# Gate projections moved into the latent attention, their logits carried through DRAM, and inverse roots spread by transposes

## The reference, cut to what matters

```python
fq, fk, fv, f_logit, c_q, c_kv, k_rope, gate_logit = split(u @ w_in)
o_fox = attention(fq, fk, fv, ...) @ w_branch_fox
q = rms_norm(heads(rms_norm(c_q) @ w_uq));  k, v = heads(rms_norm(c_kv) @ w_ukv)  # k normed with k_rope
o_mla = attention(rope(q), rope(k), v) @ w_branch_mla
g_fox, g_mla = split(sigmoid(gate_logit + b_gate))            # 1024 + 1024 columns
h = h + (g_fox * o_fox + g_mla * o_mla) @ w_out
```

## Time and profile before

| | us |
|---|---|
| median of 3 runs | 2599.38 (2598.16 to 2601.02) |
| the profiled execution | 2598.46 |
| its span, first to last instruction | 2596.3 |
| PE busy | 2433.0 (94%) |
| DVE, ACT, POOL busy | 1418.0, 948.2, 557.8 |
| mean granted TensorE clock | 0.958 of 2.4 GHz |

### The profile page before, as it was taken

The page is one execution under the profiler, slowest core; times in us unless marked ns, Lnnn a source line. Parts: engine busy times, 40 slices in busy tenths (PEclk is TensorE's granted clock), DMA queues, the critical chain, the costliest instruction groups (busy, mean ns, idle before and its releaser), DMA issues. The chain is left out here.

```text
span 2596.3 us, 37171 instructions
## 1 busy us (share of the span) xinstructions
PE 2433.0 (94%) x14204; PEld 2152.8 (83%) x14204; DVE 1418.0 (55%) x2006; ACT 948.2 (37%) x1578; POOL 557.8 (21%) x655
## 2 busy tenths in 40 slices
PE   6999999999959999978999998999998999999999
PEld 6899999999958888976777777888876888887887
DVE  7665655565456567544666662111466666655553
ACT  5333333333344445432444443111334333334332
POOL 0023300000023344231444444222310333000000
PEclk8999999999979999987998998999999999999999
DMA  4365632565230000010000002111433566326653
GB/s 183 121 209 196 209 114 95 214 227 188 101 130 1 26 26 0 1 33 7 7 7 4 3 1 81 48 49 41 163 113 104 180 221 232 133 87 255 211 197 111
DMA packets 125908, 281.13 MB, mean 108 GB/s; under 512 B 9456, under 2 KB 56432, under 8 KB 122432
## 3 DMA queue, kind: packets, MB, share of 16 engines
q1 hardware_dynamic: 125760, 279.10, 31.0%
HBM read 198.60 MB, written 80.33 MB: 107 GB/s over the span
## 5 line engine op out<-in xcount | busy, mean ns | idle before, releaser
L1068 DVE TENSOR_TENSOR f_w_lo<-f_rw,f_w_hi 128x1024 fp32r<-128x1024 f32 x154 | 203.1, 1319 | 218.7 <-ACT f_w_hi L590 218.6
L833 PE MATMUL f_ps<-u_hi,f_w_hi 128*128 128x260 f32 (+1 forms) x1056 | 283.9, 323 | 26.5 <-DVE f_w_lo L1068 13.6
L833 PE MATMUL f_ps<-u_hi,f_w_lo 128*128 128x260 f32 (+1 forms) x1056 | 282.4, 322 | 0.0
L833 PE MATMUL f_ps<-u_lo,f_w_hi 128*128 128x260 f32 (+1 forms) x1056 | 282.4, 322 | 0.0
L590 ACT CAST f_w_hi<-f_rw 128x1024 fp32r<-128x1024 f32 x154 | 161.3, 1047 | 165.1 <-PE f_ps L833 148.7
L833 PE MATMUL f_ps<-f_far_hi,f_w_hi 128*128 128x260 f32 (+1 forms) x792 | 211.8, 322 | 8.7 <-DVE f_ev L1084 8.7
L833 PEld LDWEIGHTS f_ps<-u_hi,f_w_hi 128*128 128x128 f32 x1056 | 178.0, 192 | 43.1 <-DVE f_w_lo L1068 15.4
L833 PE MATMUL f_ps<-f_far_lo,f_w_hi 128*128 128x260 f32 (+1 forms) x792 | 210.9, 321 | 0.0
L833 PE MATMUL f_ps<-f_far_hi,f_w_lo 128*128 128x260 f32 (+1 forms) x792 | 210.8, 321 | 0.0
L833 PEld LDWEIGHTS f_ps<-u_lo,f_w_hi 128*128 128x128 f32 x1056 | 177.7, 191 | 14.2
L833 PEld LDWEIGHTS f_ps<-u_hi,f_w_lo 128*128 128x128 f32 x1056 | 177.6, 191 | 14.1
(11 more groups left out here) (385 smaller groups left out, 5987.1 us busy)
## 6 DMA issues: line engine op xcount, KB each, us to landing
f_rw<-in_gu SPq DMA_DIRECT2D x88, 512.0 KB, 4.4
f_rw<-kept_dsum SPq DMA_DIRECT2D x32, 704.0 KB, 4.9
f_rw<-kept_hid SPq DMA_DIRECT2D x33, 520.0 KB, 5.7
f_rw<-in_down SPq DMA_DIRECT2D x24, 704.0 KB, 4.1
f_rw<-kept_hid SPq DMA_DIRECT2D x33, 512.0 KB, 5.5
f_gt_raw<-in_gate SPq DMA_DIRECT2D x24, 512.0 KB, 3.5
h_in<-in_wd SPq DMA_DIRECT2D x11, 1024.0 KB, 7.2
kept_dsum<-h_in SPq DMA_DIRECT2D x44, 256.0 KB, 3.1
```

Source lines behind the costliest of these rows:

```text
L833: last = nc.tensor.matmul(out[:, b, 0:N], w[:, c], u[:, b * N:(b + 1) * N], start=(j < 3 and k == 0 and i == 0), stop=(k == 3 and i == 2), ...
L1068: nc.vector.tensor_tensor(slot(w_lo, st), src, slot(w_hi, st).bitcast(F32), ALU.subtract).then_inc(wlo_done, 1)
```

## The change

`gate_phase` keeps only the branch products: the 768 matmuls of the gate logits move into the latent attention. There each head (the preparation of head 0 ahead of the loop, and that of head h+1 beside head h) gets the four logit units of one output tile, in 32 groups of three matmuls, placed by a table: one group ahead of the scores of each step, none to two behind them. They accumulate in one bank of PSUM, `GATE`, for which the projections give up one of theirs (`PROJ` has two banks, and waits for unit u-2 instead of u-3). ACT copies each finished unit out (steps 3, 6, 10 and 13), SP stores it to DRAM. The weights come in two blocks a head, split by ACT and DVE in four halves. The spread of the inverse roots becomes a transpose. Cosines, sines and the rotated key move into one tile `turn` to make room. `gate_phase` reads the logits back (1 MB a tile), splits `o` by halves and the mixed result tile by tile.

```diff
-        PROJ, BC = bank[4:7], bank[7]
+        PROJ, GATE, BC = bank[4:6], bank[6], bank[7]
-        MAXB, MT, VB = (bank[4], bank[7]), bank[5], (bank[6], bank[7])
+        MAXB, MT, VB = (bank[4], bank[7]), bank[4], (bank[5], bank[7])
+        GROUPS = {(w, x): 1 for w in range(14) for x in range(2)}
+        GROUPS.update({(2, 1): 2, (3, 1): 2, (4, 1): 2, (6, 1): 1, (11, 1): 2, (12, 1): 2, (13, 1): 0})
+        COPY_AT, HI_AT, LO_AT = (3, 6, 10, 13), {3: 2, 4: 3, 10: 0, 11: 1}, {4: 2, 5: 3, 11: 0, 12: 1}
...
+            def load_gate(p, h, i):
+                upto(sp, logit_copied, 4, p, h - 1, 2 * i + 2)
+                sp.dma_start(gate_raw[i][:, :], g.dram["logit_w"][4 * p + 2 * h + i]).then_inc(gate_in[i], 16)
+            def store_logits(p, h, j):
+                upto(sp, logit_copied, 4, p, h, j + 1)
+                sp.dma_start(g.dram["logit"][2 * p + h, j // 2, :, half(j)], logit[j % 2][:, :]).then_inc(logit_out[j % 2], 16)
...
+            def copy_logits(p, h, w):            # ACT, ahead of the exponential of step w
+                if w in COPY_AT:
+                    j = COPY_AT.index(w)
+                    upto(act, logit_ready, 4, p, h, j + 1)
+                    upto(act, logit_out[j % 2], 32, p, h, 16 * (j // 2))
+                    nc.scalar.copy(logit[j % 2][:, :], GATE[:, :]).then_inc(logit_copied, 1)
...
             def products(p, h, u):
-                out, w = PROJ[u % 3], w_head[h % 2]
+                out, w = PROJ[u % 2], w_head[h % 2]
                 if u == 0:
                     upto(pe, max_read, NM, p, h, 0)
+                    upto(pe, m_done, 1, p, h, 0)
...
                 elif u == 1:
-                    upto(pe, m_done, 1, p, h, 0)
-                elif u == 2:
                     upto(pe, v_done, 2, p, h, -1)
                 else:
-                    upto(pe, x_done, NU, p, h, u - 2)
+                    upto(pe, x_done, NU, p, h, u - 1)
...
+            def gates(p, h, w, place):
+                for q in groups(w, place):
+                    i, c, k = q // 16, q // 8 % 2, q % 8
+                    if k == 0:
+                        upto(pe, logit_copied, 4, p, h, q // 8)
+                    if c == 0 and k % 4 == 0:
+                        upto(pe, glo_done, 4, p, h, 2 * i + k // 4 + 1)
+                    x, y = slice(k * P, (k + 1) * P), columns(META + 512 * c, 512)
+                    last = mm3(nc, GATE[:, :], gate_hi[i][:, x], gate_lo[i][:, x], g.u_hi[:, k, y], g.u_lo[:, k, y],
+                               k == 0, k == KD - 1)
+                    if k == KD - 1:
+                        last.then_inc(logit_ready, 1)
...
                 for i, off in enumerate(QK_TILES[units[u][1]]):
-                    last = nc.tensor.matmul(BC[:, off:off + P], r0[:, u % 2, i:i + 1].broadcast_to([P, P]),
-                                            g.ident[:, :], start=True, stop=True)
+                    last = nc.tensor.transpose(BC[:, off:off + P], r0[:, u % 2, i:i + 1].broadcast_to([P, P]),
+                                               g.ident[:, :])
...
                     if more:
                         maxima(p, h + 1, w, 0)
+                        gates(p, h + 1, w, 0)
                     scores(p, h, w)
                     if more:
                         maxima(p, h + 1, w, 1)
+                        gates(p, h + 1, w, 1)
```

More of the change, by code:

```diff
@@ L218, in ffn_phase @@
     SN = FP * P
-    RING = 0 if first else 2 * KD
+    RING = 0 if first else 3 * KD
     if True:
@@ L2217, in pair @@
                     weights(p + 1, 0)
-                maxima_rows(p, 1)
+                around(p, 1, more=not last)
                 if not last:
                     weights(p + 1, 1)
-                    maxima_rows(p, 2)
+                    around(p, 2)
             weights(0, 0)
+            sp.dma_start(gate_raw[0][:, :], g.dram["logit_w"][0]).then_inc(gate_in[0], 16)
             weights(0, 1)
-            maxima_rows(0, 0)
+            sp.dma_start(gate_raw[1][:, :], g.dram["logit_w"][1]).then_inc(gate_in[1], 16)
+            around(0, 0)
             over_pairs(sp, pair)
+            for c in range(2):
+                sp.wait_ge(logit_out[c], 16 * 2 * HEADS)
         @block.gpsimd
@@ L2375, in sums @@
                 for i, off in enumerate(QK_TILES[c]):
-                    last = nc.tensor.matmul(PROJ[u % 3][:, SUM_AT + i:SUM_AT + i + 1], src[:, off:off + P],
+                    last = nc.tensor.matmul(PROJ[u % 2][:, SUM_AT + i:SUM_AT + i + 1], src[:, off:off + P],
                                             g.ones[0:DK, 0:1], start=True, stop=True)
@@ L2609, in pair @@
             def pair(p, last=False):
-                head(p, 0)
+                head(p, 0, next_gate=not last)
                 head(p, 1, more=not last)
+            gate_rest(0, 0, 0)
+            gate_rest(0, 0, 1)
             for w in range(NW):
@@ new lines, in gate_phase, with _, load_w, load_logits @@
+    opened, scaled, shut = sem("opened"), sem("scaled"), sem("shut")
+    uhi_done, ulo_done = sem("uhi_done"), sem("ulo_done")
+    o_tile = lambda t: (g.o_fox if t < PAIRS else g.o_mla)[:, t % PAIRS, :]
+    bank = lambda m, u: ps[2 * (m % 2) + u // 2][:, u % 2, :]
+    cut = lambda c: slice(512 * c, 512 * c + 512)
+    STACK = [g.dram["gate"][m] for m in range(KD)] + [g.dram["wout"][j] for j in range(3)]
+    @block.sync
+    def _(sp):
+        def load_w(n):
+            if n == 3:
+                sp.wait_ge(w_first_lo, 2)
+            elif n > 3:
+                sp.wait_ge(wlo_done, n - 3)
+            sp.dma_start(raw[:, n % 3, :], STACK[n]).then_inc(raw_in[n % 3], 16)
+        def load_logits(m):
+            if m >= 2:
+                sp.wait_ge(shut, 2 * (m - 1))
+            sp.dma_start(sg[:, m % 2, :, :], g.dram["logit"][m].rearrange("k p t -> p k t")).then_inc(lg_in[m % 2], 16)
+        load_w(0)
+        load_logits(0)
+        load_w(1)
+        load_w(2)
+        load_logits(1)
+        for m in range(KD):
+            load_w(m + 3)
+            if m + 2 < KD:
+                load_logits(m + 2)
@@ new lines, in _ @@
+    @block.tensor
+    def _(pe):
+        for m in range(KD):
+            for u in range(4):
+                c, first = u // 2, PAIRS * (u % 2)
+                if m == 0:
+                    pe.wait_ge(w_first_lo, u % 2 + 1)
+                elif u == 0:
+                    pe.wait_ge(wlo_done, m)
+                if m >= 2:
+                    pe.wait_ge(scaled, 4 * (m - 2) + u + 1)
+                for k in range(first, first + PAIRS):
+                    if m == 0:
+                        pe.wait_ge(olo_done, KD * c + k + 1)
+                    last = mm3(nc, bank(m, u), w_hi[:, m % 3, k * P:(k + 1) * P], w_lo[:, m % 3, k * P:(k + 1) * P],
+                               o_hi[:, k, cut(c)], o_lo[:, k, cut(c)], k == first, k == first + PAIRS - 1)
+                last.then_inc(ready, 1)
@@ L2788 @@
+    return ready, wlo_done, ulo_done, shut, scaled
 class Start:
@@ L2962, in layout @@
     branch = np.concatenate([a["w_branch_fox"][0], a["w_branch_mla"][0]])
[L2963 to L2964 removed]
+    out["gate"], gate_blocks = _k_blocks(branch), _k_blocks(gates)
+    out["logit_w"] = np.stack([gate_blocks[KD * kind + m] for m in range(KD) for kind in range(2)])
     out["wout"] = _k_blocks(a["w_out"][0])
```

341 lines of the change are left out of this document (165 added, 176 removed).

## The result

The changed kernel ("after") takes 2612.18 us (median of 15 runs, 2600.89 to 2624.80); before takes 2598.53 beside it (15 runs, 2590.56 to 2607.05). The ratio is 1.0053, its 95% interval 1.0037 to 1.0070: slower by about 14 us, where 2606 was forecast. The profiled execution of after has a span of 2612.7 us, 16.4 above that of before.

What follows compares the result with a forecast made beforehand. PE was taken as the bound: matmul count in gate_phase, waits and a lowered clock in the heads. -176 there, +168 over seven heads and +15 in head 0 made +7 us, 2606.4 beside the median; range 2575 to 2630.

Steps and rivals of the forecast that it cites:

- The groups, +21.7 a head: Latent attention: 32 groups of three matmuls, 96 at 0.226 us, add 21.7 us of PE time per head.
- The old waits covered, -4.3: Head periods: gate groups fill PE's existing waits for maxima, squares, splits and roots, saving 4.3 us a head.
- Rival E: Head periods: the groups don't cover the old waits; +30 us, 2636; chance 0.05.
- The new wait, +8.0 a head: Steps 2 to 5: projections wait for unit u-2's scaling, 1.7 us for q, 2.3 for k, two each per head.
- Rival B: Steps 2 to 5: no new projection wait, because the scaling comes in time; 2542 us; chance 0.06.
- The `GATE` bank, +0.6: Heads: the group behind a finished unit waits for ACT's copy out of the single bank; +0.6 us a head.
- The transposes, -2.0: Spread of inverse roots: 18 fewer PE instructions a head, each 0.11 to 0.14 us; -2.0 us a head.
- Rival D: Spread of inverse roots: transposes run at half their traced time; 8 us off, 2598; chance 0.03.
- Clock: left as it is on average: Seven head periods: PE's mean granted clock stays unchanged, so no time was added or removed for it.
- Head 0, +15: Head 0 prepared alone: 30.9 us added, less 8 for idle PE and 8 for its low clock; +15.
- Rival A: Steps 2 to 5 and head 0: fuller PE stays at 2.4 GHz; 27 us gained, about 2578; chance 0.25.
- Rival C: All heads: gaps, and perhaps transposes, drop the clock as in the slow heads; 2626 us; chance 0.11.

Runs made afterwards that it cites:

- e4: After, with the gate groups that stood between scores and weighing moved behind the spread, at the end of the step: 2535.56 us, ratio 0.9743.
- e6: e4 with the inverse roots spread by float32 matmuls again instead of transposes: 2542.42 us, ratio 0.9786.
- e1: Before, with two PSUM banks for the projections, which wait for the scaling of unit u-2; no gate groups: 2674.11 us, ratio 1.0283.
- e2: Before, with only the spread of the inverse roots turned into transposes: 2597.36 us, ratio 0.9993.
- e5: After, with the spread right behind the scores, ACT's copy ahead of the next Ln and Exp, DVE's scaling ahead of the next mean square: 2565.88 us.
- e7: e4 with the spread ahead of the sums, ACT's copy ahead of Ln and Exp, DVE's split and scaling ahead of the mean square: 2551.46 us.
- e8: e4 with only ACT's order changed: it copies the spread roots before the next Ln and Exp: 2527.42 us, ratio 0.9723.
- e9: The same kernel as e4, timed again beside e8: 2536.11 us, ratio 0.9753.

## Why the prediction came out as it did

It was right in direction, by 6 us too low in the median (13.65 above before against 7), and its mechanism is the measured one. In the profiled executions the difference is 16.4 us, of which 4.0 arose ahead of the attention and were nobody's forecast. By its steps:

- **`gate_phase`, -176:** measured -176.2. The start gained 1.9 us where 2.3 was worked out (ACT took 0.62 and DVE 0.70 where halves of the earlier trace rows gave 0.52 and 0.66, and the DMA 3.78 in place of 3.60). Nothing of the split of `o` showed.
- **The groups, +21.7 a head:** e4 agrees. Its periods are 59.0 us, 15.2 above the 43.8 of before, at clock 1.00. PE is idle 1.1 us less in each, and busy 16.3 more; 21.7, less 1.8 for the transposes (e6) and less 3.1 for the clock (14% of the earlier trace rows's 306.4 us, halved, over seven), is 16.8.
- **The old waits covered, -4.3:** shown; none of the earlier trace rows is left in after (3.2 us a head on the products, 5.4 on the weight loads). Rival E is out.
- **The new wait, +8.0 a head (1.7 and 2.3 us):** on the weight loads, which see the whole gap, it is 23.4 / 14 = 1.67 for q and 31.2 / 14 = 2.23 for k, 7.8 a head. On the products it is 1.43 and 1.99, since the rows let the three spreads end 0.52 us after their start and not 0.33. The way itself, 1.98 us from the spread to the product, is that worked out from the earlier trace rows. Rival B is out. e1 shows it without gates, e4 takes most of it away (13.5 us on the products in the periods, where after has 47.8).
- **The `GATE` bank, +0.6:** 3.6 us in all seven periods on the weight loads, 0.5 a head, as forecast, but only 0.9 us, 0.1 a head, on the products. In head 0 it is 2.0 us on the products, where 2.4 was put.
- **The transposes, -2.0:** nearly right as PE's own time, 1.8 a head (e6: 14.2 us over eight heads), but at a full clock a head gains only about 1 by it (7.7 us over eight), since the longer spread stood partly in waits. Alone in before the gain can't be told (e2), and there the clock falls. Rival D is out.
- **"Clock: left as it is on average":** the step that failed, by 2.4 us a head. The earlier trace rows has 0.93 of 306.4 us, 43 us at 1.2 GHz; after has 0.92 of 480.9, 77 us. Half of the 34 is 17 us, 2.4 a head (an estimate; a clock read to two digits leaves 0.5 either way). The mean hardly moves, but the stretch is longer, so the same share costs more; I had priced the clock by its mean.
- **The sum:** by the windows a period gained 3.7 us in which PE is idle and 21.2 in which it is busy, 24.9. On the products the waits give that idle part: 6.8 + 0.1 - 3.2 = 3.7. The busy part should be 21.7 - 1.8 + 2.4 = 22.3; where the 1.1 over belongs was not found. That 24.0 comes so near is in part luck: the forecast had the idle part 0.6 us too high (4.3) and the busy part 1.5 too low (19.7), and the two errors go against each other.
- **Head 0, +15:** +14.2, at 0.91 instead of 0.67. Its two deductions of 8 were rough, and both came out: PE is idle 1.7 us more there (3.2 forecast) and busy 12.5 more (11.7).

Rival A was about 25% to me, and it is what the change could have had: the clock stays full once the new wait is under its bound of 6.5 us a head. In e4 it is 13.5 / 7 = 1.9, and the clock is 1.00. I priced it at 27 us; in e4 the clock was worth about 38, and with the waits it was 77. Rival C had the right sign for the clock, not its reach: periods of 0.97 remain beside those of 0.86. Its second reason, that transposes keep the clock down, is borne out by e2 in the kernel before (0.88), if not separated from the waits, and by nothing in e4.

## What to carry to other kernels

When a buffer is taken away from a rotation, ask what stands in the queue between the last instruction on the way to its release and the one that waits for it. Here nothing did, and moving filler work by a few places, from ahead of the spread to behind it, turned a loss of 14 us into a gain of 64, without one instruction more. A reordering that closes one wait must be followed to the next user of each delayed result: e5 and e7 only moved the wait to the roots, while e8, one of their three swaps alone, brought 8 to 9 us more. And a wait is not priced by its length alone: look at the granted clock and at PE's busy time in the same window, before and after.

## What the runs showed of the hardware

Waits of 1.2 to 2.0 us on PE in the mean, four in a head period, went with a granted clock of 0.81 (e1) and 0.92 (after); waits of 0.8 us at most in the same places went with 1.00 (e4, e8). Two to three waits a head of 1.2 us in the mean and 2.3 at most, for the roots, went with 0.97 (e5, with 6.5 us of waits for the `GATE` bank besides) and 0.98 (e7). Between after and e4, 40 us of idle time came with 37 us more of busy time for the same instructions; between before and e1, 26 us with 44. So a microsecond of added idle time cost about 2 here in the one pair and 2.7 in the other. How much clock a given set of waits costs differs from one head to the next, 65.5 to 72.8 us in one execution with the same work, and the runs scatter with it: 24 us for after (15 runs), 6 and 10 for e4 and e9 (4 and 5 runs).

That the waits lower the clock is inferred from these pairs. They are not the whole of it: in e2 the clock fell from 0.93 to 0.88 while the waits summed to the same, and only the transposes and the places of the waits had changed.
